# Product-key experts: V rows gathered as 16 experts of 8 tokens, summed on four column groups in PSUM

## The reference, cut to what matters

```
q  = (h @ wq).reshape(-1, 8, 256)                 # 8 heads
s1 = q[..., :128] @ k1 ; s2 = q[..., 128:] @ k2   # 128 keys each
v1, i1 = top_k(s1, 16) ; v2, i2 = top_k(s2, 16)
sc, ci = top_k(v1[..., :, None] + v2[..., None, :], 16)
eidx = i1[ci // 16] * 128 + i2[ci % 16]           # 16 of 16384 experts
gate = softmax(sc)
z    = gelu(einsum('cd,chkd->chk', h, u_tab[eidx]))
out  = einsum('chk,chkd->cd', gate * z, v_tab[eidx])
```

## Time and profile before

| | us |
|---|---|
| median of 3 runs | 2580.36 (2579.58 to 2596.1) |
| the profiled execution | 2579.5 |
| its span | 2577.4 |
| expert part, layer 0: first U gather to the transposes of its result | 253.9 to 1056.1 |
| expert part, layer 1 | 1760.4 to 2557.8 |
| PE busy | 2064.5 (80%) |
| DVE busy | 1431.8 (56%) |
| POOL busy | 1163.8 (45%) |
| ACT busy | 539.4 (21%) |

### The profile page before, as it was taken

The page is one execution under the profiler, slowest core; times in us unless marked ns, Lnnn a source line. Parts: engine busy times, 40 slices in busy tenths (PEclk is TensorE's granted clock), DMA queues, the critical chain, the costliest instruction groups (busy, mean ns, idle before and its releaser), DMA issues.

```text
span 2577.4 us, 27554 instructions
## 1 busy us (share of the span) xinstructions
PE 2064.5 (80%) x7728; PEld 1191.4 (46%) x7728; DVE 1431.8 (56%) x3385; ACT 539.4 (21%) x1197; POOL 1163.8 (45%) x1215
## 2 busy tenths in 40 slices
PE   6998787877778777898599898779587877778777
PEld 3776532333323222575399897457232322323223
DVE  1043667777777654414751533835677777777643
ACT  2211222222222211213221211012222222222211
POOL 2000477777777776100000000004577777777772
PEclk8999888989899889998789887789898989899899
DMA  8753789999999999324000001435799999999995
GB/s 365 292 202 135 285 340 410 410 410 409 410 410 410 409 406 406 131 107 169 28 1 1 1 1 62 139 151 181 263 408 410 410 410 410 410 410 410 402 379 208
DMA packets 177203, 722.17 MB, mean 280 GB/s; under 512 B 19808, under 2 KB 20192, under 8 KB 170336
## 3 DMA queue, kind: packets, MB, share of 16 engines
q0 software_dynamic: 165888, 604.05, 59.7%
q1 hardware_dynamic: 9072, 108.80, 10.9%
q10 hardware_dynamic: 2160, 8.24, 0.8%
HBM read 715.01 MB, written 6.01 MB: 280 GB/s over the span
## 4 chain that ended last, share of the span: by engine, by line
PE 58%; DMA 24%; DVE 8%; issue 6%; ACT 2%; POOL 2%; DVEq 0%; POOLq 0%; SPq 0%; ACTq 0%
PE ps L595 27%; PE ps L509 15%; DMA ARENA<-in_peer_v,CURV 13%; DMA ARENA<-in_peer_u,CURU 9%; PE ps L715 5%; POOL ARENA L1703 2%; DMA W<-in_w_ada 1%; PE ps L697 1%; PE ps L468 1%; PE ps L478 1%; ACT DG L996 1%; PE ps L565 1%; DVE ARENA L1444 1%; DVE W L1554 1%; PE ps L791 1%
## 5 line engine op out<-in xcount | busy, mean ns | idle before, releaser
L595 PE MATMUL ps<-ARENA,DG 128*128 128x512 f32 x2304 | 1134.7, 642 | 364.5 <-ACT DG L996 247.3
L1703 POOL DMA_INDIRECT ARENA<-in_peer_u,CURU x576 | 591.8, 1027 | 1147.6 <-DVE GX L1269 951.2
L595 PEld LDWEIGHTS ps<-ARENA,DG 128*128 128x128 f32 x2304 | 447.1, 203 | 1050.9 <-issue 657.2
L1298 DVE SCALAR_TENSOR_TENSOR ARENA<-ARENA 128x1024 f32<-128x1024 f32 x576 | 703.3, 1224 | 406.8 <-DMA ARENA<-in_peer_u,CURU 404.7
L1703 POOL DMA_INDIRECT ARENA<-in_peer_v,CURV x576 | 556.2, 966 | 228.7 <-issue 138.6
L996 ACT ACTIVATE DG<-ident,CF 128x128 f32<-128x128 f32 x576 | 219.4, 398 | 807.9 <-PE ps L595 705.6
L509 PE MATMUL ps<-H,W 128*128 128x288 f32 x1024 | 258.2, 415 | 2.8 <-DVEq L1632 2.8
L509 PEld LDWEIGHTS ps<-H,W 128*128 128x128 f32 x1024 | 198.7, 195 | 58.3 <-DVEq L1632 3.0
L715 PE MATMUL ps<-W 128*128 128x128 f32 (+1 forms) x1088 | 128.4, 283 | 0.0
L715 PEld LDWEIGHTS ps<-W 128*128 128x128 f32 (+1 forms) x1088 | 126.2, 197 | 2.3 <-issue 0.9
L509 PE MATMUL ps<-ARENA,W 128*128 128x288 f32 x512 | 127.0, 412 | 0.0
(11 more groups left out here) (252 smaller groups left out, 1635.5 us busy)
## 6 DMA issues: line engine op xcount, KB each, us to landing
W<-in_w_ada SPq DMA_DIRECT2D x24, 2048.0 KB, 11.3
W<-in_peer_wq SPq DMA_DIRECT2D x8, 2048.0 KB, 8.2
W<-in_conv_w_in SPq DMA_DIRECT2D x6, 2048.0 KB, 14.6
ARENA<-in_peer_u,CURU POOLq DMA_INDIRECT x576, 6.6
ARENA<-in_peer_v,CURV POOLq DMA_INDIRECT x576, 6.6
W<-in_conv_w_out SPq DMA_DIRECT2D x2, 2048.0 KB, 10.1
W<-in_rwkv_wr SPq DMA_DIRECT2D x2, 2048.0 KB, 13.0
W<-in_rwkv_wk SPq DMA_DIRECT2D x2, 2048.0 KB, 9.7
```

Of the source, the lines that this page charges most:

```text
L595: m = pe.matmul(ps[:, 4 + 2 * e + i, :], DG[:, k % NDIAG, :], RVV[:, k % RING, i * 512:(i + 1) * 512], start=(k == 0), stop=(k == TOPK - 1))
L1298: v.scalar_tensor_tensor(RU[:, k % RING, :], RU[:, k % RING, :], 1.0, h, ALU.mult, ALU.mult, accum_out=ZB[:, e, k:k + 1]).then_inc(s_z, 1)
L1703: pool.indirect_dma_start(ring[:, k % RING, :], None, tab, bass.IndirectOffsetOnAxis(ap=idx[:, k:k + 1], axis=0)).then_inc(landed[k % RING ...
```

## The change

- A V gather now brings the 16 experts of 8 tokens instead of one expert of 128 tokens. To get the indices into this order, DVE spreads them (`spread_indices`, one 128x128 product with a constant mask), PE multiplies with a constant (`regroup_indices`, 16 columns), and DVE writes them as `CURV` (`v_indices`). A constant array of 272 columns is loaded at the program's start for this.
- The coefficients go the same way: gelu times gate, spread over 128 columns (`spread_coefs`), a matmul with the constant (`regroup_coefs`), and then `place_coefs`, one DVE instruction of 512 columns from PSUM, that fills `ST`, 16 stationary matrices of 128x32. ACT's 16 diagonal matrices for each unit are gone.
- A matmul has 32 output columns. Four of them, on the four column groups of the array, belong to one batch of four V slots, so a unit has four batches. `v_free` is counted up once for each batch, by 4.
- PSUM sums over all heads of a token tile (units 0 to 7, 8 to 15, 16 and 17). ACT copies it into `OACC` (`expert_rows`) at the end of a tile; DVE's add for each unit and its clearing of `OACC` are gone.
- Only four query tiles lie in the V slots' arena, the other 12 lie in a slot of `W`. V slots 4 to 7 are free from the start, and V(u,0) to V(u,3) are put there (`v_slot`). In layer 0 the `W` slot is one that the tiles of `ad9` come through, so these wait for the last scores.
- The two loops on each engine are written out, without the counting of steps that they needed (`s_go`, `s_selgo`, `s_actgo`).
- In unit 0 DVE goes to z(1,0) at once; units 2 and 3 are chosen between the z of unit 1. The transposes of h for the later tiles come after PE's unit 0.

```diff
-                        m = pe.matmul(ps[:, 4 + 2 * e + i, :], DG[:, k % NDIAG, :],
-                              RVV[:, k % RING, i * 512:(i + 1) * 512], start=(k == 0), stop=(k == TOPK - 1))
-                    m.then_inc(v_free, 1)
+            for lu in range(UNITS):
+                u = u0 + lu
+                regroup_coefs(u)
+                if lu + 1 < UNITS:
+                    regroup_indices(u + 1)
+                if lu % 8 == 0:
+                    pe.wait_ge(acc_free, 2 * (3 * layer + lu // 8))
+                pe.wait_ge(s_st, u + 1)
+                for q in range(TOPK // BATCH):
+                    for i in range(2):
+                        for j in range(BATCH):
+                            k = BATCH * q + j
+                            if i == 0:
+                                pe.wait_ge(v_land[v_slot(k)], u * 32 + 16 * (k // RING + 1))
+                            m = pe.matmul(ps[QUAD * j:QUAD * (j + 1), 4 + i, :], ST[:, k, :],
+                                  RVV[:, v_slot(k), i * 512:(i + 1) * 512], start=(lu % 8 == 0 and q == 0),
+                                  stop=(lu in TILE_ENDS and q == 3), skip_group_check=True)
+                    m.then_inc(v_free, BATCH)
...
+                    for k in range(TOPK):                      # DVE, unit(lu)
+                        if k == 2:
+                            spread_coefs(u)
+                            if 0 < lu and lu + 2 < UNITS:
+                                choose_ends(u + 2)
+                        if k == 3:
+                            spread_indices(u + 1)
+                        if k == 5:
+                            place_coefs(u)
+                            v_indices(u + 1)
...
+                        z_of(u + 1, k)
...
                 for k in range(TOPK):                          # POOL, experts(layer)
-                    get_u(u0, k, 0)
-                for k in range(RING):
-                    get_u(u0 + 1, k, 1)
-                pool.wait_ge(bank_ready, GROUP[f"sc{layer}"] + 9)
+                    get_u(0, k)
+                for k in range(BATCH):
+                    get_v(0, k)
+                for k in range(12):
+                    get_u(1, k)
+                for k in range(BATCH, TOPK):
+                    get_v(0, k)
+                    if k < 2 * BATCH:
+                        get_u(1, k + 8)
...
         weight_tiles(a["peer_wq"][0:4], GROUP["qa0"], 4)
         later_queries(0)
+        tiles[WT["q0"]] = (tiles[WT["q0"]][0], GROUP["sc0"] + 8)
```

More of the change, by code:

```diff
@@ L28 @@
 RING = 8
-NDIAG = 4
+BATCH = 4
+TILE_ENDS = (7, 15, 17)
 WRING = 4
@@ L550, in experts @@
                     for half in range(2):
-                        m = pe.matmul(o[:, (2 * h + half) * P:(2 * h + half + 1) * P], Q[:, 2 * h + half, 0:P], KT[:, half, h, :],
+                        m = pe.matmul(o[:, (2 * h + half) * P:(2 * h + half + 1) * P], Q4[:, 2 * h + half, 0:P], KT[:, half, h, :],
                                       start=True, stop=True)
                 done(m)
-                project(f"qb{layer}", f"q{layer}", 12, H, 4)
+                for m in range(4, 16, 4):
+                    project(f"qb{layer}", f"q{layer}", 4, H, m, m - 4)
+                    if m == 4:
+                        regroup_indices(u0)
                 pe.wait_ge(s_q, 16 * (layer + 1))
@@ L564, in experts @@
                                 h = 4 * h4 + j
-                                m = pe.matmul(o[:, j * P:(j + 1) * P], Q[:, 2 * h + half, tile * P:(tile + 1) * P],
+                                m = pe.matmul(o[:, j * P:(j + 1) * P], query_of(layer, 2 * h + half)[:, tile * P:(tile + 1) * P],
                                               KT[:, half, h, :], start=True, stop=True)
@@ L945, in experts @@
                 u0 = layer * UNITS
+                SCALL = scores(layer)
                 def gate_exp(u):
@@ L1205, in _, with choose @@
             residual("cout", 0)
-            def choose(u, e, layer):
+            def choose(u, layer):
+                e, lu = u % 2, u - layer * UNITS
                 state = {"j": 0}
@@ L1214, in step @@
                     state["j"] += 1
-                    if not isinstance(u, int) or u * NSEL + j + 1 - back > 0:
+                    if u * NSEL + j + 1 - back > 0:
                         v.wait_ge(s_sel, u * NSEL + (j + 1 - back))
-                    v.sem_inc(s_selgo, 1)
                     make().then_inc(s_sel, 1)
-                s0, s1 = SCUR[:, e, 0, :], SCUR[:, e, 1, :]
+                s0, s1 = (SCUR[:, lu, 0, :], SCUR[:, lu, 1, :]) if lu < 2 else (scores(layer)[:, lu, 0:NKEYS], scores(layer)[:, lu, NKEYS:])
                 r0, r1 = REST[:, 0, 0:NKEYS], REST[:, 1, 0:NKEYS]
@@ L1365, in experts, with ends @@
-                with v.Fori(0, UNITS // 2 - 2) as i:
-                    for e in range(2):
-                        unit(i * 2 + (u0 + e), i * 2 + e, e, 0)
-                for lu in range(UNITS - 4, UNITS):
-                    unit(u0 + lu, lu, lu % 2, lu - (UNITS - 4))
-                v.wait_ge(acc_free, u0 + UNITS + 2)
-                v.sem_inc(s_acc, 1)
+                def ends(u):
+                    choose_ends(u)
+                    yield
+                for lu in range(UNITS):
+                    unit(lu)
@@ L1750, in _ @@
+                for lu in range(1, UNITS):
+                    for k in range(TOPK):
+                        get_v(lu, k)
+                        if lu + 1 < UNITS:
+                            get_u(lu + 1, k)
             experts(0)
```

289 lines of the change are left out of this document (150 added, 139 removed).

## The result

| | before | after |
|---|---|---|
| median of 4 runs each | 2579.97 us | 2723.94 us |
| range of the runs | 2575.63 to 2596.10 | 2713.38 to 2733.29 |
| ratio, 95% interval | | 1.0545 [1.0485, 1.0604] |
| span of the profiled execution | 2577.4 | 2731.3 |

The change makes the kernel 5.5% slower. The forecast was 2611 us, 1.2% slower, with a range up to 2662. The direction was right; the time lies outside the range.

A forecast was written before the change was run, and what follows sets the result against it. The prediction took the DMA, full at 410 GB/s in both expert parts, as the bound, with POOL having little time in hand. Sum: 2579.5 - 24 (starts) + 75 (steady units) - 20 (ends) = 2610.5, median 2611 us; range 2535 to 2662.

The forecast's parts named there:

- What bounds the kernel: Both expert parts: DMA full at 410 GB/s, 40.95 us a unit; POOL has only 1.3 us a unit to catch up.
- The steady ring: Steady units: V(u,8) waits 4.0 us for `ST` and the first batch; period 43.7 us against 40.95, together +75 us.
- 25 x 1.24: Steady units: POOL's 25 gathers from V(u,8) to U(u+2,4) at 1.24 us each, added to a 12.7 us way back.
- bound of 46.6 us for the period: Steady units: upper bound of the period, with gathers of 1.33 us and landings of 7.2.
- If they meet POOL's gathers, POOL's issue gets longer ... that is in the upper bound: DVE's four new instructions a unit, 0.3 to 0.7 us: costed at nothing, longer POOL issue left to the upper bound.
- The third rival: POOL slows too: DVE's two-operand products and fetches lengthen gathers; period 45.3 us, 51 us more, 2662 us; chance 0.13.
- Starts, -24: Start of both layers' expert parts: V(1,0) 13.4 and 14.4 us earlier, 4 charged for `ad9` loads: -24 us.
- Ends, -20: End of both expert parts, V(17,0) to the transposes: 30.3 us instead of 41.7 and 39.2, -20 us.
- Addresses at nothing: V gathers: the same rows in another order, taken to cost nothing.
- Unrolling, nothing to gain: Written-out units: a cited rule says they gain, but the loops already run at the DMA's 40.95 us, so nothing.
- Landing 6.6: Steady units: a gather takes 6.6 us from issue to landing, one part of the 12.7 us way back.

The follow-up runs named there:

- e1: The change with `ST` written ahead of z(u+1,3) and the index spread ahead of z(u+1,2), two z and a choose step earlier for `ST`: 2555 us.
- e6: The kernel of e1 with h of all units but 0 and 1 left in PSUM, where z reads it: 2556 us.
- e2: The change with `CURV` written from `IDX` as before, so a V gather brings one expert of 128 tokens again: 2716 us.
- e4: The kernel before with its four loops written out and nothing else: 2661 us.
- e7: The kernel of e4 with DVE's add to `OACC` moved behind z(u+1,0) of the next unit: 2585 us.
- e5: The kernel of e1 with POOL's V(u,8) also waiting for z(u+1,6) in units 1 to 16 of each layer: 2765 us.
- e9: The kernel before, loops kept, with POOL's V(u,8) also waiting for z(u+1,6) in units 1 to 16 of each layer: 2780 us.
- e3: The change with z's h operand read from PSUM instead of SBUF from unit 2 of each layer on: 2660 us.

## Why the prediction went wrong

- *What bounds the kernel* (410 GB/s, POOL 1.3 us a unit in hand): right. e1 and e6 come back to within 0.5 us a unit of that bound. The 1.3 us in hand are what the old U gathers lose to z: 16 x 0.08.
- *The steady ring*: right in place and cause, in all of the steady units. z, step, `ST`, the batch of 3.5 us at 1.2 GHz and the hand-offs came as summed, and the way back from U(u+1,4) to V(u,8) took 12.5 us instead of 12.7. The idle time beyond the usual 0.3 us was 3.0 instead of 4.0, because the seven gathers between took 9.4 instead of 8.7 and the landings less (6.0 us, below).
- *25 x 1.24*: this is the term that failed. It takes every gather of POOL at its quickest, 0.94 us and 0.30 between two, as if DVE's z could not hold one up. From V(u,8) to U(u+2,4) it took 34.7 us on the mean of the 13 units instead of 31.0; even before it was 32.0, with the 1.28 of the earlier trace rows. By the whole unit: the 32 gathers of a unit took 18.5 + 16.0 = 34.5 us instead of 30.1: 4.4 us a unit more, less 0.8 of idle time (12.8 instead of 13.6), is the 3.6 between 47.3 and 43.7. The two stretches of the table are 53 and 55 us over their forecast, 108 in all; starts and ends add 17 and the middle takes 3 away. The whole miss is 123 us in the profiled execution and 113 in the medians. The bound of 46.6 us for the period is passed as well, and the range of the time, which ends at 2662, had not been drawn from it: 46.6 would have given some 2700.
- *"If they meet POOL's gathers, POOL's issue gets longer ... that is in the upper bound"*: I looked at the new DVE instructions and not at z, the old one, which is 1.22 us long 16 times a unit, and had no account of what a pause does to the step between z and the gathers. The rows had it: U gathers of 1.02 beside V gathers of 0.94 in every pair, and gathers of 1.62 and 1.95 us at the starts, where the engines aren't in step yet. The third rival had the effect and part of its reason (DVE's products of two operands lengthen the gathers), at 45.3 us a period, less than half of its size; it got a chance of 0.13.
- *Starts, -24*: -12.4. Layer 0's scores ended at 306.7, forecast 305.1. V(1,0) came 36.2 us behind them instead of 30.3, with gathers of 1.4 to 1.9 us where DVE does z after z, and 5.4 us of waiting for PE at V(0,12), which I had seen as following at once:

```profile
310.78 1.88 POOL L1761 DMA_INDIRECT ARENA<-in_peer_u,CURU  x1 [4.08 <-DVE ARENA L1360]
...
317.17 1.65 POOL L1761 DMA_INDIRECT ARENA<-in_peer_v,CURV  x1 [0.31 <-PE ps L646]
...
337.72 0.93 POOL L1761 DMA_INDIRECT ARENA<-in_peer_v,CURV  x1 [5.40 <-PE ps L646]
```

- *Ends, -20*: -14.5, 32.05 and 34.35 us instead of 30.3; the V gather at V(17,0) alone took 1.69 and 1.63.
- *Addresses at nothing*: held (e2). *Unrolling, nothing to gain*: there was nothing; the rule cited there, by which the edit would gain, isn't borne out by e4 or e7. A loss of 81 us in the old DVE order was possible (e4), and I had no bound for it.
- *Landing 6.6*: the queue view of 600 to 900 us shows 6.0 in the changed kernel, so even the pace behind the pause didn't bring 6.6 back:

```profile
q14 instruction: 5, 0.04, 0.0%
issues: line engine op xcount, KB each, median us to landing
ARENA<-in_peer_v,CURV POOLq DMA_INDIRECT x101, 6.0
ARENA<-in_peer_u,CURU POOLq DMA_INDIRECT x101, 6.0
```

## What to carry to other kernels

Where POOL issues the gathers and DVE works on them with two SBUF operands, look in the timeline for a steady phase between the two: a kernel that runs at the DMA's pace may do so only because each of DVE's instructions starts just behind a gather. Then a pause costs more than its length (3.0 us a unit became 6.3 in the change, 4.4 became 6.4 in e5, 4.7 became 5.9 in e9), and 0.2 us less in a loop cost 2.5 us a unit (e4's 44.1 against e7's 41.6); put anything that a full ring waits for as early as its inputs allow, and price a wait with the gathers at their colliding length as well. Here the remedy was to write `ST` two z earlier, which turned 5.5% slower into 1.1% faster [0.9824, 0.9947].

## What the runs showed of the hardware

- An indirect gather of 128 rows takes POOL 0.94 us, or 0.80 us and the rest of a DVE instruction that has two SBUF operands and is under way at its start (560 of the 564 such gathers with over 0.15 us of it left, in before, the change and e4). With one operand in PSUM the DVE instruction is as long (1.22 us) and the gather isn't held up (e3, 176 of 177).
- The DVE side didn't pay: z lasts 1.22 us on the mean whether a gather is under way at its start or not (167 and 35 z of the change from 400 to 1000 us; the longest is 1.28, and it is one of the latter).
- The busy tenths of the DMA say 9 at 353 GB/s as at 410: over 600 to 900 us the window view gives a share of 0.95 for 353 GB/s in the change and, before, 1.03 for 410.
- Sixteen instructions on four column groups took 3.6 us at the lower clock in the units, as the row at the program's start had it.
